# Odd mixer's latent tokens first, the last pair of each step one step later, expert 1's rows selected on chip and thirteen weight buffers in the second mixture

## What is computed

```
for l in range(2):
    h_lat = modulate(x_lat, norm_mix_g[l], sh1, sc1)      # RMS norm, scale, shift
    h_ctx = modulate(x_ctx, norm_mix_g[l], csh1, csc1)
    ...                                                   # l = 0: even mixer; l = 1: odd mixer
    x_lat = x_lat + g1 * o_lat
    h_lat = modulate(x_lat, norm_ffn_g[l], sh2, sc2)
    ...                                                   # l = 0: the same for x_ctx
    y = moe(...)                                          # l = 0: 512 tokens, l = 1: 256
    x_lat = x_lat + g2 * y_lat                            # l = 0: x_ctx too

def odd_mixer(h_lat, h_ctx, w_in, w_out, qg, kg, cos, sin, need_ctx_out):
    q, k, v = split_cols(h_lat @ w_in, SIZES_ODD)         # 1024, 256, 256 columns
    q = apply_rope(rms_norm(q, qg), cos, sin) * 128 ** -0.5
    k = apply_rope(rms_norm(k, kg), cos, sin)
    ck, cv = split_cols(h_ctx @ w_in[:, 1024:], SIZES_ODD[1:])
    ck = rms_norm(ck, kg)
    return block_attention(q, [ck, k], [cv, v]) @ w_out   # only latent queries

def moe(h, ...):                                          # 16 experts, each token has two
    y = sum(comb[:, e:e+1] * ((silu(h @ w1[e]) * (h @ w3[e])) @ w2[e]) for e in range(16))
```

## Time and profile before

| | us |
|---|---|
| median of three runs | 1717.12 |
| lowest, highest | 1713.95, 1723.39 |
| the profiled execution | 1723.89 |
| its span | 1722.3 |
| TensorE busy in it | 1550.1 |

### The profile page before, as it was taken

One profiled execution on the slowest core, in us unless ns is written; L12 is line 12 of the kernel. 1 busy time (PEld: TensorE's weight loads), 2 busy tenths in 40 slices (PEclk: granted clock), 3 DMA queues, 4 the chain that ended last, 5 costly groups with the idle time before them and its releaser, 6 DMA issues.

```text
span 1722.3 us, 27159 instructions
## 1 busy us (share of the span) xinstructions
PE 1550.1 (90%) x11454; PEld 1106.9 (64%) x11454; DVE 577.3 (34%) x1410; ACT 341.9 (20%) x784; POOL 94.1 (5%) x145
## 2 busy tenths in 40 slices
PE   6999999999889999997887799999669996999897
PEld 5787678877634856645436699998545674555554
DVE  2514422333245248206314111111065633233233
ACT  1223211122141123125213000000142213100000
POOL 0010000100110000002001000000100001000000
PEclk8899999999989999998998899999879997999999
DMA  8365443556764431225422799999772124899996
GB/s 258 84 216 181 139 144 112 187 172 198 209 209 138 131 98 50 90 82 176 145 78 114 273 399 395 403 395 400 269 270 73 74 74 152 322 385 398 394 391 249
DMA packets 181401, 367.21 MB, mean 213 GB/s; under 512 B 18988, under 2 KB 137608, under 8 KB 164800
## 3 DMA queue, kind: packets, MB, share of 16 engines
q1 hardware_dynamic: 164640, 322.90, 52.6%
q0 software_dynamic: 10624, 32.74, 6.0%
q10 hardware_dynamic: 6048, 10.31, 1.7%
HBM read 345.52 MB, written 20.41 MB: 212 GB/s over the span
## 4 chain that ended last, share of the span: by engine, by line
PE 77%; DVE 8%; DMA 8%; ACT 4%; issue 2%; POOL 1%; SPq 0%; POOLq 0%; ACTq 0%; DVEq 0%
PE ps_proj L635 30%; PE ps_outp L635 10%; PE ps_proj L1199 7%; PE ps_outp L1199 7%; PE ps_score L1199 7%; DMA ring<-in_exp_w 4%; PE ps_outp L1144 3%; PE ps_turn L788 2%; PE ps_outp L1301 2%; DMA h_t<-in_exp_w 1%; PE ps_proj L761 1%; PE ps_score L806 1%; DVE probs L2101 1%; PE ps_score L635 1%; DMA arena<-expert_in 1%
## 5 line engine op out<-in xcount | busy, mean ns | idle before, releaser
L635 PE MATMUL ps_proj<-h_t,ring 128*128 128x256 f32 (+1 forms) x1280 | 363.4, 444 | 13.6 <-ACT h_t L1740 8.1
L635 PEld LDWEIGHTS ps_proj<-h_t,ring 128*128 128x128 f32 x1280 | 252.5, 199 | 119.8 <-issue 84.9
L1199 PE MATMUL ps_proj<-ring,arena 128*32 128x128 f32 (+2 forms) x1824 | 128.0, 391 | 4.4 <-ACT arena L1898 2.5
L1199 PE MATMUL ps_outp<-ring,arena 128*32 128x384 f32 (+3 forms) x1600 | 125.8, 419 | 3.9 <-DVE arena L2482 3.2
L1199 PE MATMUL ps_score<-ring,arena 128*32 128x384 f32 (+2 forms) x1824 | 123.3, 381 | 4.7 <-DMA ring<-in_exp_w 4.7
L1199 PEld LDWEIGHTS ps_proj<-ring,arena 128*32 128x32 f32 (+1 forms) x1824 | 110.5, 117 | 22.1 <-issue 13.0
L1199 PEld LDWEIGHTS ps_score<-ring,arena 128*32 128x32 f32 (+1 forms) x1824 | 102.9, 114 | 25.4 <-issue 12.8
L1199 PEld LDWEIGHTS ps_outp<-ring,arena 128*32 128x32 f32 (+1 forms) x1600 | 89.5, 117 | 32.4 <-DVE arena L2482 5.8
L635 PE MATMUL ps_proj<-ring,h_t 128*128 128x256 f32 (+1 forms) x512 | 106.4, 366 | 0.4 <-ACT arena L1766 0.4
L1586 ACT ACTIVATE arena<-ps_proj 128x512 f32<-128x512 f32 (+1 forms) x68 | 39.0, 576 | 325.0 <-PE ps_proj L635 323.5
L635 PEld LDWEIGHTS ps_proj<-ring,h_t 128*128 128x128 f32 x512 | 92.7, 192 | 14.9 <-issue 3.6
(11 more groups left out here) (336 smaller groups left out, 1779.4 us busy)
## 6 DMA issues: line engine op xcount, KB each, us to landing
ring<-in_exp_w SPq DMA_DIRECT2D x152, 1024.0 KB, 11.1
ring<-in_ada_w SPq DMA_DIRECT2D x48, 1024.0 KB, 5.5
ring<-in_w_in SPq DMA_DIRECT2D x30, 1024.0 KB, 6.2
arena<-in_exp_w SPq DMA_DIRECT2D x30, 1024.0 KB, 18.3
ring<-in_even_w_in SPq DMA_DIRECT2D x12, 1024.0 KB, 7.4
h_t<-in_exp_w SPq DMA_DIRECT2D x10, 1024.0 KB, 19.7
ring<-in_w_out SPq DMA_DIRECT2D x8, 1024.0 KB, 5.3
expert_in<-arena POOLq DMA_DIRECT2D x1, 6144.0 KB, 31.0
```

Of the source, the lines that this page charges most:

```text
L635: last = pe.matmul(out, w, a, start=(i == 0), stop=(i == len(pairs) - 1))
L1199: last = pe.matmul(b[p0:p0 + pn, c0:c0 + wn], x_of(p0, lo, pn), w[:, w0:w0 + wn], start=first and p0 not in strip[:i], stop=done and p0 no ...
```

## The change

Four things are done.

- **Token order.** `TOKEN_BLOCKS = (2, 3, 0, 1)` sets the order of the gathers, of ACT's and DVE's mixing, of the transposes and of the residual: latent blocks first. The norm is done in two halves, the latent one first. TensorE sums the latent half ahead of the last block's transposes, and the context half behind step 0 of the mixer. A new semaphore `ctx_ready` tells step 4 that the context is there.
- **The pair one step late.** The pair (sum of squares, rotation) of step c, now `turn_pairs(c)`, is issued behind the matmuls of step c+1; that of step 5 behind the token-major values. ACT takes the roots (`head_root`) one step late too.
- **Expert 1's rows.** DVE writes a second 0/1 matrix, and TensorE selects expert 1's rows as it does expert 0's, between up 0 and gate 1. POOL's first load is now that of expert 2.
- **Thirteen places.** `EXTRA` is 7: new are `row_store` (a buffer of the even mixer), the context half of `x_t` (whose eight pieces of 256 columns take a block in two DMAs, 1 KB a piece), and the two buffers of the attention's probabilities, now one tensor `both_probs`. Five blocks are issued ahead of the output weights. The block in `x_t` waits for `xn_ready` of the context half, the one in `both_probs` for the end of the odd attention.

```diff
-EXTRA = 4
+EXTRA = 7
...
-        EARLY = EXTRA - 1
-        extra = [arena[:, 4 * D:6 * D], arena[:, 6 * D:8 * D], arena[:, 2 * D:4 * D], h_t[:, KC * S:2 * KC * S]]
+        EARLY = EXTRA - 2
...
+        extra = [arena[:, 4 * D:6 * D], arena[:, 6 * D:8 * D],
+                 row_store[:, :, :].rearrange("p k t -> p (k t)")[:, 0:SLOT], arena[:, 2 * D:4 * D],
+                 x_t[:, :, 0:S], h_t[:, KC * S:2 * KC * S], both_probs[:, :]]
...
+        TOKEN_BLOCKS = (2, 3, 0, 1)
...
             experts(0)
-            b = claim("proj")
-            for s in range(2):
-                for k in range(KC):
...
-            sum_quarters(T2)
+            for i in range(3):
+                mixed_turned(i)
+            norm(h2[:, :, S:T2], S)(0, 4)
+            mixed_turned(3)
             ready = mixer_input()
+            def turn_pairs(c):
+                head_sums("ones", g_sq)
+                got("proj", mark["raw", c])
+                b = claim("outp")
+                chain(b[:, :], [(cst("rot2"), raw[:, c % 2, :])]).then_inc(filled["outp"], 1)
...
-                k_raw = mark["raw", c] = use["proj"]
-                head_sums("ones", g_sq)
-                got("proj", k_raw)
-                b = claim("outp")
-                chain(b[:, :], [(cst("rot2"), raw[:, c % 2, :])]).then_inc(filled["outp"], 1)
+                mark["raw", c] = use["proj"]
+                if c == 0:
+                    norm(h2[:, :, 0:S], S)(0, 4)
+                if c >= 1:
+                    turn_pairs(c - 1)
             mark["gv_slot"] = slot[0]
             token_major(h2, 4)
-            got("proj", use["proj"])
+            k_gv = use["proj"]
+            turn_pairs(5)
+            got("proj", k_gv)
...
-            rms_root(T2)
-            shift(h2, 1, 0, T2)
+            stream_squares(0, mark["moe_done", 0] - 4)
+            rms_root(S)
+            stream_shift(0)
+            stream_squares(1, mark["moe_done", 0])
             for c in range(6):
+                if c == 1:
+                    rms_root(S)
+                    stream_shift(1)
...
-                head_root(8 + c, P, c >= 4)
+                if c >= 1:
+                    head_root(8 + c - 1, P, c - 1 >= 4)
             for t in (0, 2):
                 evac(gv[:, t:t + 2, :])
+            head_root(13, P)
...
+                    for t in range(NB):
+                        ins = dve.tensor_scalar(pick_first[:, NB + t, :], cst("slot"), place_of[:, t, 1:2], None, ALU.is_equal)
+                    ins.then_inc(second_ready, 1)
...
-                rows_turned(1)
+                pe.wait_ge(second_ready, 1)
+                selected_rows(1)
...
-                pool.dma_start(x_rows[0:CAP[l], :], first_of(xrow_d, l, 1)).then_inc(x_loaded, 16)
+                pool.dma_start(x_rows[0:CAP[l], :], first_of(xrow_d, l, l + 1)).then_inc(x_loaded, 16)
...
                 elif i == 2:
+                    sp.wait_ge(mod_ready, DEPTH)
+                elif i == 3:
                     sp.wait_ge(filled["turn"], mark["moe_done", 0])
-                elif i == 3:
+                elif i == 4:
+                    sp.wait_ge(xn_ready, 3 * 2 * KC)
+                elif i == 5:
                     sp.wait_ge(*slot_end[mark["gv_slot"]])
+                elif i == 6:
+                    sp.wait_ge(filled["outp"], mark["odd_attention"])
```

More of the change, by code:

```diff
@@ L1210, in expert_weights @@
                     pe.wait_ge(loaded, value)
[L1211 removed]
+                    w, per = pieces(w), 4 if kind == "out" else 2
+                    return lambda k: lambda w0, wn: w[:, k * per + w0 // S, :]
                 def used_up(kind, e, f):
@@ L2940, in weights_load @@
                     src = w.rearrange("e (k p) n -> p (e k) n", p=P)[:, 2 * q:2 * q + 2, :]
-                sp.dma_start(dst.rearrange("p (k n) -> p k n", k=4 if c < 4 else 2), src).then_inc(done, 16)
+                if len(dst.shape) == 2:
+                    sp.dma_start(dst.rearrange("p (k n) -> p k n", k=4 if c < 4 else 2), src).then_inc(done, 16)
+                    return
+                rows = 2 if c < 4 else 1
+                for half in range(2):
+                    part = src[:, rows * half:rows * half + rows, :]
+                    if c < 4:
+                        part = part.rearrange("p k n -> p (k n)").rearrange("p (j c) -> p j c", c=S)
+                    else:
+                        part = part[:, 0, :].rearrange("p (j c) -> p j c", c=S)
+                    sp.dma_start(dst[:, 4 * half:4 * half + 4, :], part).then_inc(done, 16)
             def block_load(n, i):
```

131 lines of the change are left out of this document (76 added, 55 removed).

## The result

| | before | after |
|---|---|---|
| median, us | 1715.53 (1708.5 to 1723.39, 4 runs) | 1694.64 (1690.9 to 1702.68, 4 runs) |
| ratio of after to before | | 0.9883, 95% interval 0.9846 to 0.9921 |
| the profiled execution, its span | 1723.89, 1722.3 | 1694.8, 1693.2 |

The change makes the kernel 20.9 us faster; 1698 was predicted, with a gain of 18.9. The median is in the range of 1688 to 1708.

What follows compares the result with a forecast made beforehand. TensorE held 77% of the chain, idle before the odd mixer, in its steps and in the second mixture, whose end the weights held. Mixer 6.6 + mixture 12.3 = 18.9 us off the 1717.1 median: 1698 us, range 1688 to 1708.

Steps and rivals of the forecast that it cites:

- Latent tokens first: Gather to odd mixer: latent half's norm ready sooner, first matmul at 1262.6 instead of 1273.5, 10.9 us earlier.
- The pair one step late: Odd mixer: steps 8.7 us instead of 9.58; last pair uncovered, 5.5 us gap, attention 9.1 us earlier, not 15.6.
- The clock behind the gap: Attention: TensorE's clock falls after standing 5.5 us, costing 2.5 us, bounds 0 and 6.
- rival (d): Attention: clock stays down after the gap, all 16 units cost 32 us, kernel slower at 1728; chance 0.04.
- The second mixture: Second mixture: 8.4 + 6.4 - 2.5 = 12.3 us gained, weights still setting the end; TensorE alone would allow 18.7.
- Gate 0 to gate 1's end: Second mixture's start: expert 1's rows selected on chip, gate 1 at full clock, ending 9.5 us earlier.
- The three blocks and the pieces: Second mixture's weights: three blocks fewer to load save 8.4 us; seven blocks in 1 KB pieces cost 2.5.
- the hole of 8 x (1 - 79/393) = 6.4 us closes: Weight stream, 1466 to 1474: moves 79 GB/s against 393; gate 1's buffers come free earlier, gaining 6.4 us.
- The stalls that stayed: Second mixture's experts: some 6 us of TensorE stalls on weight blocks were to stay.
- (a): Second mixture: weights don't hold the end, TensorE's 18.7 us count in full, kernel at 1689; chance 0.17.
- (b): Mixer and mixture: later step 0, clock costs attention 6, hole stays open; 1709 to 1706; chance 0.12.
- (c): Second mixture's first experts: probabilities block or its followers late, 8.4 us gone, kernel at 1706; chance 0.03.

Runs made afterwards that it cites:

- e8: Changed kernel with only half of each second- or later-round weight block loaded, output not the reference's: 1698.71 us, 0.9879 of the kernel before.
- e3: Changed kernel with ten buffer places instead of thirteen: 1699.13 us, 0.9902 of the kernel before.
- e6: Changed kernel with ten places and expert 1's rows from DRAM, so only the odd mixer's part: 1709.93 us, 0.9959 of the kernel before.
- e2: Changed kernel with the last pair put back ahead of the token-major values: 1685.25 us, 0.9826 of the kernel before.
- e9: Changed kernel with the last pair ahead of the token-major values, repeated in another batch: 1696.48 us, 0.9855 of the kernel before.
- e1: Changed kernel run again, unedited: 1693.96 us, 0.9876 of the kernel before.
- e11: Changed kernel run once more, unedited, as base of the last batch: 1701.23 us, 0.9902 of the kernel before.
- e12: Changed kernel with expert 1's rows loaded from DRAM, no on-chip selection, thirteen places kept: 1703.07 us, 0.9907 of the kernel before.
- e7: Second mixture's part alone (thirteen places, expert 1's rows selected on chip) with the odd mixer of before: 1705.73 us, 0.9932 of the kernel before.
- e4: Changed kernel with all second-mixture blocks in 1 KB pieces, two DMAs each: 1724.88 us, 1.0044 of the kernel before.

## Why the prediction came out right

**Latent tokens first: right.** First matmul predicted at 1262.6; it is at 1259.00 + 3.9 = 1262.9. Step 0 took 7.50 us, not 8.8: the granted clock came back sooner than in the profile before. That isn't of the change: the same instructions took 8.83 us in e8, 10.13 in e3, and in e6 10.15:

```profile
1261.49 10.15 PE L644 MATMUL ps_proj<-h_t,ring 128*128 128x256 f32 x32 [1.74 <-ACT h_t L2019]
```

The norm in TensorE's row takes 2.15 us (1266.43 to 1268.58), 2.2 predicted.

**The pair one step late: right.** Steps of 8.62 us (8.7 predicted). DVE's last product of a step ends at 1283.72 and ACT's next copy starts at 1284.31: it fits by 0.6 us. The gap of 5.67 us (5.5 predicted) is real, by e2 and e9.

**The clock behind the gap: right kind, too large.** The granted clock was 0.63 in 1332 to 1338 and 1.00 from 1338 on. From the scores to the output projection it took 45.03 us instead of 44.08: 0.95 us lost, not 2.5, and far from rival (d). The Trainium skill (TensorE: Matmul & The Clock Gate, the section on cycling through PSUM queues) tells of groups with small idles that switch between the rates again and again; here 1338 to 1344 is at full rate with 0.81 us idle in 6, and so are the stretches behind it up to 1378, so the trace doesn't show it. Together with step 0 the mixer gave 9.5 us in the profile, 6.6 predicted, and e6 gives 8.7 in the median.

**A term that was missing.** In the profile after, the first selection and gate 0 took 12.4 us in sum, before 10.8, and the way to gate 0 became 2.0 us longer, all of it in the selection (6.62 us, before 4.63). I had not asked what the idle time of 1.55 us ahead of the selection does. In e1, e2, e9 and e11 the same instructions took 7.5 us; e11's:

```profile
1423.67 3.79 PE L646 MATMUL ps_turn<-arena 128*128 128x64 f32 x32 [1.55 <-DVE arena L2656]
1427.39 3.67 PE L1210 MATMUL ps_proj<-arena 128*64 128x256 f32 x32
```

In after, e3 to e8 and e12 they took 12.3 to 12.4. Both happen to one and the same kernel (after; e1 and e11), so it isn't of the change; what decides it stays open. Of these 4.9 us only part reaches the end: behind the weights' issue after takes 0.5 us more than e1 and 3.4 more than e11, for where TensorE starts sooner it waits longer for weights later (loss 7.4 and 6.3 us, not 2.6).

**The second mixture: 12.3 predicted, 12.9 measured (e7), but the steps behind it were off.** Gate 0 to gate 1's end was right: 9.7 us earlier, 9.5 predicted. The three blocks and the pieces agree: 8.4 - 2.5 = 5.9, e3 gave 5.2 (not clear of noise) and e4 the pieces' price. The failed step is "the hole of 8 x (1 - 79/393) = 6.4 us closes". It was read from one stretch of one execution. These are four stretches from gate 0 on (20, 8, 32 and 180 us; the last value is GB/s), in before, after, and e6.

```profile
1445.90:1465.90 20.00, 11.16 (x76) 6.97 (x77) 0.94 (x3) 2.65 (x5) 4.16 (x5) 0.67 0.87 316
1465.90:1473.90 8.00, 7.70 (x44) 4.69 (x46) 0.42 (x1) 0.94 (x3) 0.54 (x1) 0.66 0.32 82
1473.90:1505.90 32.00, 30.77 (x252) 18.03 (x250) 9.58 (x20) 2.86 (x8) 1.02 (x2) 1.00 1.00 372
1505.90:1685.90 180.00, 166.70 (x1321) 95.36 (x1315) 53.57 (x112) 15.71 (x44) 5.63 (x11) 1.00 1.02 393
```

```profile
1434.60:1454.60 20.00, 19.70 (x157) 13.40 (x158) 1.36 (x4) 3.58 (x7) 2.77 (x4) 0.89 0.90 341
1454.60:1462.60 8.00, 7.68 (x67) 4.66 (x65) 3.07 (x7) 0.66 (x2) 0.54 (x1) 1.00 1.05 400
1462.60:1494.60 32.00, 30.77 (x246) 17.57 (x242) 9.64 (x20) 2.85 (x8) 1.02 (x2) 1.00 1.02 389
1494.60:1674.60 180.00, 171.26 (x1367) 98.75 (x1367) 55.26 (x116) 16.47 (x46) 5.09 (x10) 1.00 1.02 389
```

```profile
1440.30:1460.30 20.00, 16.84 (x108) 10.42 (x108) 0.94 (x3) 2.90 (x6) 3.23 (x5) 0.71 0.89 309
1460.30:1468.30 8.00, 7.70 (x64) 4.52 (x65) 1.58 (x4) 0.69 (x2) 0.00 (x0) 1.00 1.01 384
1468.30:1500.30 32.00, 30.77 (x253) 17.92 (x247) 10.89 (x23) 2.86 (x8) 1.02 (x2) 1.00 1.01 382
```

Within 60 us of gate 0 before has moved 20 x 316 + 8 x 82 + 32 x 372 = 18.9 MB, after 22.5: 3.6 MB, or 9.2 us at 391 GB/s, not 6.4. That is a main reason why the stage gave 17.6 us in the profiles. The stalls that stayed, 2.6 us, seem to be fewer than the 6 predicted, but e1 and e11 have 7.4 and 6.3. And e6, with the same second mixture as before, moved 21.5 MB in these 60 us; the changed kernel moved 22.0 in e1 and 22.2 in e11. So 2.6 MB, or 6.6 us, of before's hole belonged to that one execution. And it shows where the difference between 29.1 us (profiles) and 20.9 (medians) lies: 3.9 us came ahead of the change, and before's profile, 1723.9, lay 3.5 to 8.4 us above its medians, with the wait of 8.70 us in it. The hole was sized too small for the profiled execution and is probably too large for a usual one; that 12.3 met 12.9 owes something to luck. The shares don't add up closely either: places 5.2 and selection 1 to 6 make 6 to 11 of 12.9, and 2 to 7 us stay without a run that shows them. Counted by profiles, the stage from gate 0 on takes 262.5 us in e6 and 253.6 to 256.5 in the changed kernel, 6 to 9 less, where before's single profile makes it 15 to 18.

**The rivals.** (a), that the weights don't hold the end, is nearly true: e8 gained nothing measurable without them, and of the 18.7 us that TensorE alone would allow, 9.7 + 6.6 = 16.3 came between the two profiles. But between the medians it was 12.9, so the time did not end at 1689. (b), (c) and (d) did not happen: the first matmul was on time, no early block was late, and the clock came back within 5 us.

## A version that beats both

The changed kernel with the last pair ahead of the values (e2, e9) has 0.9826 [0.9788, 0.9864] and 0.9855 [0.9832, 0.9879] to the kernel before, 30 and 25 us, and is below the changed kernel in both batches.

## What to carry over

Moving dependent work one step later pays per step, but its last instance loses its cover: put that one back ahead of the last big piece of independent work, which here was worth at least as much as the 4.4 us of the rest of that edit. Weight buffers were worth about the blocks that they save from streaming, less what their layout costs per block (5.9 us reckoned, 5.2 measured, not clear of noise). And a wait behind a small round trip through DRAM that runs beside bulk loads is no constant: one profile may hold a long one, so compare its time with the medians before a term is taken from it. Compare parts of profiles from a common event on, too: here the point where the changed part begins moved by 16 us from one execution to the next.

## What the runs showed of the hardware

- Loads in 1 KB pieces run at 343 GB/s where the same blocks in longer pieces have 389 to 393, over 180 us and with the DMA engines as full as they get (e4 against after and before; share 1.09 against 1.02).
- POOL's scatter (four issues) is done 3.2 us after the last one when no weight block is issued meanwhile, and 11.4 us after it when blocks are (e6, e11; in the other profiles it follows the order in which the blocks come).
- After the same idle of 1.55 us with the same instructions ahead, TensorE's next 32 records took 3.79 us in some executions and 6.4 to 6.9 us in others (e1, e2, e9, e11; after, e3 to e8, e12). What picks one of them no run shows.
- After 5.67 us of idle TensorE was back at the full clock (1.00) within 5 us of work, in an attention with small idles throughout (after, 1332.97 to 1338).
- Executions of one kernel differ by far more ahead of a stretch than in it: the weights' issue lies between 1247.8 and 1263.8 us, while the changed kernel takes 437.7 to 441.1 us behind it (after, e1, e11).
